# Two attention mixers of a fused block, one head at a time against pairs of heads on halves of TensorE

## The reference, cut to what matters

```python
def stick_breaking_attention(q, k, v):      # per head, causal; written per block of 128 queries in the reference
    z = (q @ k.T) * 64 ** -0.5
    log_not = where(s < t, log_sigmoid(-z), 0)
    between = cumsum(log_not, reverse=True) - log_not
    a = where(s < t, exp(log_sigmoid(z) + between), 0)
    return a @ v

def retention(q, k, v, log_gamma):          # q and k rotated (apply_rope); chunks of 128, here in its direct form
    return (q @ k.T * 64 ** -0.5 * exp((t - s) * log_gamma) * (s <= t)) @ v

y_c = silu(r_g) * head_group_norm(retention(...), ret_norm_g)
branches = [y_a, y_b, y_c]                  # each @ w_branch, times sigmoid(gates), summed, @ w_out
```

## Time and profile before

| | us |
|---|---|
| median of 3 runs (lowest, highest) | 4114.14 (4106.35, 4119.47) |
| the profiled execution, its own time | 4115.26 |
| its span in the profile | 4113.5 |
| TensorE busy | 3909.2 |
| VectorE busy | 1782.7 |
| ScalarE busy | 1496.2 |
| GpSimd busy | 251.2 |

### The profile page before, as it was taken

How to read it: one execution, slowest core, us unless ns; L and a number is a source line. 1 busy time by engine, 2 the same in 40 slices (tenths; PEclk the granted TensorE clock), 3 DMA queues, 4 the chain that set the end, 5 groups by cost and what they waited for, 6 DMA issues and landing times.

```text
span 4113.5 us, 45373 instructions
## 1 busy us (share of the span) xinstructions
PE 3909.2 (95%) x18892; PEld 3158.6 (77%) x18892; DVE 1782.7 (43%) x2714; ACT 1496.2 (36%) x2379; POOL 251.2 (6%) x199
## 2 busy tenths in 40 slices
PE   7998889999998999999899999999998999999998
PEld 6898768888887977887667658878876775787887
DVE  5427635544533165545463333343335444334332
ACT  4245423322323264323444333242334443223232
POOL 0000010000000001000000001110110000012011
PEclk9999999999999999999999999999999999999999
DMA  5320012333322122232111122323221111232222
GB/s 195 109 92 2 31 62 84 114 114 109 113 68 80 64 68 77 93 102 91 59 43 61 47 67 93 103 86 99 96 81 37 62 57 59 80 102 88 98 98 82
DMA packets 110430, 335.80 MB, mean 82 GB/s; under 512 B 11664, under 2 KB 28432, under 8 KB 110096
## 3 DMA queue, kind: packets, MB, share of 16 engines
q1 hardware_dynamic: 110224, 332.90, 24.6%
HBM read 329.18 MB, written 2.10 MB: 81 GB/s over the span
## 4 chain that ended last, share of the span: by engine, by line
PE 88%; DVE 6%; ACT 4%; issue 1%; DMA 1%; POOL 0%; SPq 0%; DVEq 0%; ACTq 0%
PE ps L585 64%; PE ps L621 6%; PE ps L604 2%; PE ps L669 2%; PE ps L1206 1%; PE ps L1104 1%; PE ps L630 1%; PE ps L1213 1%; PE ps L1027 1%; PE ps L1015 1%; PE ps L1006 1%; PE ps L978 1%; PE ps L840 1%; PE ps L1154 1%; PE ps L813 1%
## 5 line engine op out<-in xcount | busy, mean ns | idle before, releaser
L2019 DVE TENSOR_TENSOR wlo<-raw,whi 128x1024 fp32r<-128x1024 f32 (+3 forms) x655 | 746.4, 1144 | 1099.4 <-ACT whi L1291 1098.3
L1291 ACT ACTIVATE whi<-raw 128x1024 fp32r<-128x1024 f32 (+3 forms) x655 | 627.1, 967 | 812.5 <-PE ps L585 636.4
L585 PE MATMUL ps<-bh,whi 128*128 128x512 f32 x1248 | 494.0, 396 | 1.6 <-ACT rv L1890 1.6
L585 PE MATMUL ps<-bh,wlo 128*128 128x512 f32 x1248 | 486.1, 389 | 0.8 <-DVE wlo L2019 0.8
L585 PE MATMUL ps<-bl,whi 128*128 128x512 f32 x1248 | 485.8, 389 | 0.0
L585 PE MATMUL ps<-ah,whi 128*128 128x512 f32 (+2 forms) x1424 | 420.8, 355 | 14.3 <-ACT whi L1291 14.3
L585 PE MATMUL ps<-ah,wlo 128*128 128x512 f32 (+2 forms) x1424 | 418.5, 353 | 0.9 <-DVE wlo L2019 0.8
L585 PE MATMUL ps<-al,whi 128*128 128x512 f32 (+2 forms) x1424 | 416.6, 352 | 0.0
L585 PEld LDWEIGHTS ps<-ah,whi 128*128 128x128 f32 x1424 | 246.0, 189 | 52.6 <-ACT whi L1291 16.5
L585 PEld LDWEIGHTS ps<-bh,whi 128*128 128x128 f32 x1248 | 234.2, 188 | 55.9 <-issue 5.9
L585 PEld LDWEIGHTS ps<-bl,whi 128*128 128x128 f32 x1248 | 234.3, 188 | 51.7 <-issue 3.8
(11 more groups left out here) (350 smaller groups left out, 6474.7 us busy)
## 6 DMA issues: line engine op xcount, KB each, us to landing
raw<-weights_d SPq DMA_DIRECT2D x543, 512.0 KB, 3.3
raw<-weights_d SPq DMA_DIRECT2D x48, 256.0 KB, 2.6
raw<-weights_d SPq DMA_DIRECT2D x48, 192.0 KB, 2.4
x<-nab_d SPq DMA_DIRECT2D x24, 256.0 KB, 2.7
x<-x_t_d SPq DMA_DIRECT2D x4, 1024.0 KB, 6.0
dt<-rtab_d SPq DMA_DIRECT2D x16, 256.0 KB, 3.0
raw<-weights_d SPq DMA_DIRECT2D x16, 128.0 KB, 2.0
out_d<-x SPq DMA_DIRECT2D x4, 512.0 KB, 2.9
```

The costliest lines, as they stand in the source:

```text
L585: m = e.matmul(p[:, 0:n], tiles(w, i)[:, k, :], xs[:, x0 + k, c0:c0 + n], start=pi == 0 and k == 0 and ti == 0, stop=i == job and k == kt ...
L1291: e.activation(flat(WHI, j), raw(j), ACT.Copy).then_inc(q.did("hi", j))
L2019: e.tensor_tensor(flat(WLO, j), raw(j), flat(WHI, j).bitcast(F32), ALU.subtract).then_inc(q.did("lo", j))
```

## The change

- Queries and keys of stick breaking stay in plain tiles of two heads (`KS` in place of `KZ`); so do the rotated keys of retention (`RK` for `RKZ`). The zero fills go. A score product of head b contracts over partitions 64 b to 64 b + 63 only, and the products of the two heads alternate and write to different banks.
- The value products of the two heads alternate too, into the two halves of one bank.
- Stick breaking on TensorE for pair j: scores of both heads, a projection (next queries), values of pair j - 1, rest of the first head, a projection (next keys), rest of the second head. Beside the last pair stand the first two projections of retention.
- Retention for pair j: mean of j - 1, score groups 0 and 1, a projection, variance of j - 1, values of groups 0 and 1, score group 2, a projection, rotation of the next queries, values of group 2, rotation of the next keys, the gate projection. `RAT` has four buffers of 2 KB and `RAS` goes; score groups take banks 6, 7 and 5, 2. The last pair is spread over the first column tile of gates and branches by `last_tiles()`.
- ScalarE, VectorE and SyncE follow that order. SyncE fetches the decay tables of pair j when score group 2 of pair j - 1 has been used by both heads.

```diff
             S("w_in_2", (l,), 0, 8, plain(IN_OFF[3] + 128 * j), (7,))
-            S("w_in_2", (l,), 0, 8, plain(IN_OFF[4] + 128 * j), (5,))
+            S("w_in_2", (l,), 0, 8, plain(IN_OFF[4] + 128 * j), (7 if j else 5,))
+        for o in (6, 7):
+            S("w_in_2", (l,), 0, 8, plain(IN_OFF[o]), (7,))
         moving("w_in_2", (l,), D, IN_OFF[8], 512, (0, 1, 2, 3))
         for j in range(4):
             for b, o in enumerate((6, 7, 9)):
-                S("w_in_2", (l,), 0, 8, plain(IN_OFF[o] + 128 * j), (b,))
+                if j or b == 2:
+                    S("w_in_2", (l,), 0, 8, plain(IN_OFF[o] + 128 * j), (b,))
...
-            def sb_scores(h):
-                j, b = h // 2, h % 2
-                q.wait_ge(("sbq", l, j), ("sbk", l, j), ("kz0", l, j % 2), ("kz1", l, j % 2))
+            def sb_scores(j):
+
+                q.wait_ge(("sbq", l, j), ("sbk", l, j))
                 for x, kts in enumerate(SBT):
-                    p, o = bank(3 * (h % 2) + x, ("sba", l, h, x)), 0
+                    ps, o = [bank(3 * b + x, ("sba", l, 2 * j + b, x)) for b in range(2)], 0
                     for kt in kts:
                         n = TL - 128 * kt
-                        m = e.matmul(p[:, o:o + n], KZ[j % 2][:, b, 128 * kt:128 * kt + 128], QS[j % 2][:, 128 * kt:],
-                                     start=o == 0, stop=False, skip_group_check=True)
+                        for b in range(2):
+                            r = slice(64 * b, 64 * b + 64)
+                            m = e.matmul(ps[b][:, o:o + n], KS[j % 2][r, 128 * kt:128 * kt + 128], QS[j % 2][r, 128 * kt:],
+                                         start=o == 0, stop=False, skip_group_check=True)
                         o += n
-                    m.then_inc(q.did("sbs", l, h, x))
+                    m.then_inc(q.did("sbs", l, j, x))
...
+            def sb_values(j):
+
+                o = bank(6, ("sbol", l, j))
                 for x, kts in enumerate(SBT):
-                    o = 0
+                    c = 0
                     for kt in kts:
                         n = TL - 128 * kt
...
+                        q.wait_ge(("sba", l, 2 * j, x), ("sba", l, 2 * j + 1, x), ("sv", l, kt))
+                        for b in range(2):
+                            h = 2 * j + b
+                            m = e.matmul(o[64 * b:64 * b + 64, 128 * kt:], SV[:, kt, 64 * h:64 * h + 64],
+                                         sb_at(h, x)[:, c:c + n], start=kt == 0, stop=kt == 3, skip_group_check=True)
+                        c += n
+                    m.then_inc(q.did("sbv", l, j, x))
+
+            for _ in range(2):
                 lin("w_in_2", B, br, ONE)
...
+            for j in range(4):
+                sb_scores(j)
+                lin("w_in_2", B, br, ONE)
+                if j:
+                    sb_values(j - 1)
+                sb_rest(2 * j)
+                lin("w_in_2", B, br, ONE)
+                sb_rest(2 * j + 1)
+            sb_values(3)
...
+            def ret_scores(j, x):
+
+                q.wait_ge(("rq", l, j), ("rk", l, j))
+                ps, o = [bank(((6, 7), (5, 2))[x % 2][b], ("ra", l, j, x, b)) for b in range(2)], 0
+                for kt in SBT[x]:
+                    w = TL - 128 * kt
+                    for b in range(2):
+                        r = slice(64 * b, 64 * b + 64)
+                        m = e.matmul(ps[b][:, o:o + w], RK[j % 2][r, 128 * kt:128 * kt + 128], RQ[j % 2][r, 128 * kt:],
+                                     start=True, stop=True, skip_group_check=True)
+                    o += w
+                m.then_inc(q.did("rs", l, j, x))
+
+            def ret_values(j, x):
+
+                p = bank(4, ("ryc", l, j)) if x == 0 else PS[4]
+                o = 0
+                for kt in SBT[x]:
+                    w = TL - 128 * kt
+                    q.wait_ge(("ra", l, j, x, 0), ("ra", l, j, x, 1), ("rv", l, kt))
+                    for b in range(2):
+                        h = 2 * j + b
+                        m = e.matmul(p[64 * b:64 * b + 64, 128 * kt:], RV[:, kt, 64 * h:64 * h + 64],
+                                     ret_at(b, x)[:, o:o + w], start=kt == 0, stop=kt == 3, skip_group_check=True)
+                    o += w
+                m.then_inc(q.did("rpv", l, j, x))
+
+            def ret_mean(j):
                 p = bank(3, ("rdev", l, j))
                 q.wait_ge(("ryc", l, j))
                 e.matmul(p, BONES, RY[0], start=True, stop=True, skip_group_check=True).then_inc(q.did("rmean", l, j))
-                yield
+
+            def ret_var(j):
                 p = bank(3, ("rln", l, j))
                 q.wait_ge(("rsq", l, j))
                 e.matmul(p, BONES, RY[1], start=True, stop=True, skip_group_check=True).then_inc(q.did("rvar", l, j))
+
+            rotate(6, ("rq", l, 0), PR, RAW2[0], ("rraw", l, 0, 0))
+            rotate(7, ("rk", l, 0), PR, RAW2[1], ("rraw", l, 0, 1))
+            lin("w_in_2", B, br, ONE)
+            for j in range(3):
+                if j:
+                    ret_mean(j - 1)
+                ret_scores(j, 0)
+                ret_scores(j, 1)
+                lin("w_in_2", B, br, ONE)
+                if j:
+                    ret_var(j - 1)
+                ret_values(j, 0)
+                ret_values(j, 1)
+                ret_scores(j, 2)
+                lin("w_in_2", B, br, ONE)
+                rotate(0, ("rq", l, j + 1), PR, RAW2[0], ("rraw", l, j + 1, 0))
+                ret_values(j, 2)
+                rotate(1, ("rk", l, j + 1), PR, RAW2[1], ("rraw", l, j + 1, 1))
+                lin("w_in_2", B, br, ONE)
+
+            def last_tiles():
+                ret_mean(2)
+                ret_scores(3, 0)
+                ret_scores(3, 1)
+                yield "first gate"
+                ret_var(2)
+                ret_values(3, 0)
+                ret_values(3, 1)
+                ret_scores(3, 2)
+                yield "first branch"
+                ret_values(3, 2)
                 yield
...
+                yield "second gate"
+                ret_mean(3)
+                yield "second branch"
+                ret_var(3)
+
+            last = last_tiles()
...
+            sb_queries(0)
+            sb_keys(0)
+            for j in range(4):
+                sb_scores(2 * j)
+                sb_queries(j + 1) if j < 3 else ret_raw(0, 0)
+                sb_scores(2 * j + 1)
+                sb_rest(2 * j)
+                if j:
+                    sb_values(j - 1)
+                sb_keys(j + 1) if j < 3 else ret_raw(0, 1)
+                sb_rest(2 * j + 1)
+            sb_values(3)
...
+            ret_gate(0)
+            for j in range(3):
+                if j:
+                    ret_square(j - 1)
+                ret_raw(j + 1, 0)
+                if j:
+                    ret_scale(j - 1)
+                ret_raw(j + 1, 1)
+                if j:
+                    ret_high(j - 1)
+                ret_out(j)
+                ret_gate(j + 1)
...
+            def ret_decay(j, x):
+
                 for b in range(2):
...
+                    o = 0
+                    q.wait_ge(("rs", l, j, x), ("rtab", l, 2 * j + b),
+                              *([("rpv", l, j, 0)] if x == 2 else [("rpv", l, j - 1, 2)] if j else f))
+                    for kt in SBT[x]:
+                        w = TL - 128 * kt
+                        m = e.tensor_tensor(ret_at(b, x)[:, o:o + w], PS[((6, 7), (5, 2))[x % 2][b]][:, o:o + w],
+                                            DT[b][:, 0:w], ALU.mult)
+                        o += w
+                    m.then_inc(q.did("ra", l, j, x, b))
...
+            ret_rotate(0, 0)
+            ret_rotate(0, 1)
+            chunk("w_in_2")
+            for j in range(3):
+                if j:
+                    ret_dev(j - 1)
+                ret_decay(j, 0)
+                ret_decay(j, 1)
+                chunk("w_in_2")
+                if j:
+                    ret_norm(j - 1)
+                ret_decay(j, 2)
+                chunk("w_in_2")
+                ret_rotate(j + 1, 0)
+                ret_rotate(j + 1, 1)
+                if j:
+                    ret_low(j - 1)
+                chunk("w_in_2")
+
+            def last_tiles():
+                ret_dev(2)
+                ret_decay(3, 0)
+                ret_decay(3, 1)
+                yield "first gate"
+                ret_norm(2)
+                ret_decay(3, 2)
+                yield "first branch"
+                ret_low(2)
                 yield
...
+                yield "second gate"
+                ret_dev(3)
+                yield "second branch"
+                yield
+                ret_norm(3)
+                ret_low(3)
+
+            last_ = last_tiles()
...
-            weights(at_sv + 4 + LOOK + 3)
+            weights(at_sv + 7)
             decay(0, *fence(f"end_sb{l}"))
             for j in range(1, 4):
-                weights(at_sv + 4 + 3 * (j + 1) + LOOK + 1)
```

(25 more changed lines are left out.)

264 lines of the change are left out of this document (63 added, 201 removed).

## The result

| | before | after |
|---|---|---|
| median, us (runs) | 4110.58 (4) | 4010.94 (4) |
| lowest to highest | 4106.35 to 4119.47 | 4004.28 to 4013.23 |
| profiled execution, its span | 4113.5 | 4002.5 |

The ratio is 0.9752, with a 95% interval of 0.9731 to 0.9774. The medians lie 99.6 us apart; the forecast was 99 (4015 us, of a range of 4004 to 4048). That the changed kernel takes 4011 and not 4015 us comes from the base: with one more run the median of the kernel before is 4110.58, 3.6 us under the one that I had.

A forecast was written before the change was run, and what follows sets the result against it. TensorE's product length was taken as the bound, its waits as a small second purse. Per layer 8.1 + 8.3 + 29.4 + 5.0 - 1.3 = 49.5 us, 99 for two, took 4115.3 to 4016, stated as 4015 us; range 4004 to 4048.

The forecast's parts named there:

- change of form: TensorE switching between array shapes (row halves, column halves, whole array): 0.19 us each, range 0.10 to 0.25.
- 1. Scores: Stick-breaking scores: eight blocks of 2.26 us become four pair blocks of 2.5 us, a gain of 8.1 us a layer.
- 2. Values: Stick-breaking values: eight blocks of 2.29 us become four of 2.5 us, a gain of 8.3 us a layer.
- 3. Retention: Retention pairs, with their tile waits and half clock: 51.8 us become 22.4, a gain of 29.4 us a layer.
- 4. Waits that go: TensorE waits for key copies, around suffix sums, for retention value copies and before the variance product go: 5.0 us a layer.
- 5. The wait that comes: First stick-breaking pair: TensorE reaches the suffix sums at 8.0 us, their inputs at 9.3; a loss of 1.3 us a layer.
- What I had costed at nothing: VectorE fills, second head's ScalarE chain, retention's output-tile and gate copies, and DMA: covered, zero cost; a failure costs 3.4 plus 2.6 us.
- The chain of the second head: Stick breaking, first pair: ready 16.6 us after the scores start, before TensorE reaches its sums at 17.1, so no wait.
- new waits in order (B): Second head's or output tile's chain comes late once in each stage and layer: 24 us, giving 4039 us; chance 0.20.
- Serial wide halves (C): Wide halves of scores and values run one after the other: 68 us over two layers, giving 4083 us; chance 0.05.
- Loads that are not hidden (D): Weight loads of the column halves, 137 ns each, are exposed: at most 35 us, giving 4050 us; chance 0.04.
- Slower (E): Stick-breaking pairs bound by their chain, not TensorE, each waiting over 12.4 us; 4127 us at 14 us a pair; chance 0.02.

The follow-up runs named there:

- full-height run: The changed kernel, but scores of both mixers contract over all 128 partitions again, with the other head's keys zero; 4041.38 us, ratio 0.9841.
- in-turn runs: The changed kernel, but in stick breaking all products of a pair's first head precede the second's: for scores 4018.87 us, for values 4026.91 us.
- before_attention_first: The kernel before, but the last retention pair's attention comes ahead of the norm of the pair before it; 4102.75 us, ratio 0.9994.

## Why the prediction was right, point by point

Two projections lie now in stick breaking instead of retention. They take 5.67 us behind half-array products (2210.35 to 2216.02), and I take 11.2 for both. The part of the stretch up to the projection of retention's values went from 133.99 to 126.80 us with them in, a gain of 18.4; the forecast for its steps was 8.1 + 8.3 + 2.7 - 1.3 = 17.8. The rest went from 178.25 to 135.11, a gain of 43.1 - 11.2 = 31.9; the forecast was 29.4 + 0.8 + 1.5 = 31.7.

The size of a change of form was forecast at 0.19 us from small products and came out at 0.14 to 0.18 on the wide ones.

1. Scores: four blocks of 2.35 us are 9.4 against 18.1, 8.7 gained, less what the change costs the product behind (an array-wide product just behind halves is 0.1 us late in several rows: suffix sums start to start 0.97 and 0.86). About 8.3, forecast 8.1. That row halves carry it is shown by the full-height run. The stage with its two further projections was forecast at 105 us and took 104.9.
2. Values: four blocks of 2.30 are 9.2 against 18.3, 9.1 less 0.4, forecast 8.3. The phrase "two passes of 1,280 columns at 2.4 GHz are 2.13 us" left out that each f32 pass takes two cycles a column (512 columns in 0.43 us here, 0.23 in a projection's fp32r pass); the 2.26 us of the row had shown it, and all durations were taken on that footing.
3. Retention: 5.0 us a pair in its own blocks and some 0.4 on the neighbours, forecast 5.6. No stretch of half clock is left (1.00 in both stretches above). The share of the row halves is shown by the full-height run. No run takes away the column halves here or splits them from the fewer changes of form (seven for sixteen); for those the account rests on the rows.
4. Waits that go: all named ones went; TensorE's idle time fell by 8.7 us a layer. The forecast had 5.0 here and 4.8 in step 3, less 1.3 of step 5, 8.5 in all.
5. The wait that comes: 1.3 forecast, 1.2 measured, from 9.34 us (2186.04 to 2195.38) of the first head's chain. It went when a second projection was put ahead of it, so its cause is shown.

What I had costed at nothing was nothing: neither the decayed tiles, nor the gate's copy, nor a DMA stands in the list of waits. The chain of the second head was forecast to end 16.6 us after the scores start; its last row sum on VectorE ends at 2202.36, 16.3 us after, and TensorE comes for it at 2204.43. That this is cover and not luck is shown for stick breaking alone, where taking it away cost 62 us; retention's order was not tried so.

The rivals: new waits in order (B) did not come. Serial wide halves (C) are what the in-turn runs come near to, 3.86 and 3.96 us a block. Loads that are not hidden (D) did not come either: sixteen loads of 137 ns are 2.2 us, and the values' block is 2.30 us with its passes. By the Trainium skill, TensorE: Matmul & The Clock Gate, Part 3, loads of column halves, which share their rows, should not overlap running products, though the same part also lets a load go ahead when it fills the background weight buffer. These rows speak against the first and don't test the second. Full-array products speak against it too: the 24 of a projection start 0.23 us apart with a load of 189 ns each. Slower (E) needed 14 us a pair of waits; even without projections between, the pairs waited 26.2 us a layer in all.

## What to carry to other kernels

When two heads of 64 are multiplied one after the other, put them on row halves for scores and on column halves for values, with the heads' products alternating, or in turns of at most four f32 passes a head (0.1 us a pair at most here), and keep changes of form few (0.14 to 0.18 us each here). The halves free TensorE's time, and with it the cover that hid the chains of the other engines: move independent products between a head's scores, its sums and its values, or more than half of the gain can turn into waits and half clock (62 of 99 us here). To judge an edit of one or two us in a kernel of 4000, measure the stretch between two fixed products in the trace and not the median.

## What the runs showed of the hardware

- TensorE starts a pass on a free half before passes of the other half that stand ahead of it in the program, up to four places: a second head's first pass started with the fifth, first and third pass of the first head when it stood ninth, fifth and seventh (2232.41, 2331.30 and 2221.48 us). The lengths fit: 2.30 + 1.49 = 3.79 us for the first, which took 3.86, and 2.30 + 0.91 = 3.21 for the last, which took 3.22. What sets the four places, and whether it is four passes or two products, is not shown. The Trainium skill, TensorE: Matmul & The Clock Gate, Part 3, says that products start and end strictly in order; with products on two halves these starts differ from that. Whether the ends keep an order is not shown, since ends are modelled.
- A change of form cost 0.14 to 0.18 us. Between halves and full array it is (2.35 - 2.13 + 0.1) / 2 = 0.16 for a scores block and (2.30 - 2.13 + 0.1) / 2 = 0.14 for a values block; between row and column halves 0.17 in the run that alternates groups; and one change less saved 0.18. The Trainium skill, TensorEngine Tiling (Array Packing), Key Properties, names the drain and gives no size.
- Behind waits of 3.4, 4.6 and 6.9 us the granted clock stood at 0.50 (the row is from the kernel before, behind the wait of 3.4); in the changed kernel and in `before_attention_first`, whose longest waits were 1.2 and 1.5 us, it stayed at 1.00 in this stretch. In the latent attention, ahead of the stretch, it fell behind a shorter one: the changed kernel has a wait of 2.2 us there, up to 2139.95, and a granted clock of 0.53 from 2140.50 to 2143.50.

```profile
2443.40:2450.10 6.70, 5.54 (x9) 1.87 (x10) 2.18 (x5) 2.01 (x2) 0.00 (x0) 0.50 0.00 0
```
